# Differential attention: the step's probabilities are turned before the value products and the turned output

## The chip, the cores and the metric

The kernel runs on one core of one Trainium2 chip, as one launch. The metric is the device time of that launch in microseconds. Five engines run their own instruction streams in order and meet through semaphores: PE (TensorE, matrix products; PEld is its weight load), ACT (ScalarE), DVE (VectorE), POOL (GpSimd) and SP (SyncE, which issues the transfers of weights).

## What is computed

The reference is a stack of four blocks on 512 positions with 256 context positions, width 1024. The change lies in the mixer of the second one, differential attention with 8 heads. Each head has two query and key halves m = 0, 1 of 64 columns and one value of 128 columns, and the output uses the difference of the two softmaxes:

```python
def _diff_core(q, k, v, lam, sub_g, lam_init):
    b, nq, h, _, d = q.shape
    s = jnp.einsum('bqhmd,bkhmd->bhmqk', q, k).astype(jnp.float32) * d ** -0.5
    p = jax.nn.softmax(s, axis=-1)
    a = (p[:, :, 0] - lam * p[:, :, 1]).astype(v.dtype)
    o = jnp.einsum('bhqk,bkhe->bqhe', a, v)
    o = _rms_norm(o, sub_g) * (1.0 - lam_init)
    return o.reshape(b, nq, h * v.shape[-1])
```

The keys are the 512 positions and the 256 context positions, 768 in all; the queries are the 512 positions. The output product with `w_out`, the residual and the MLP follow.

## The kernel before

The program is one list of phases (norms, linear layers, attention, scans, fast products), and each engine has a function of its own that walks through it. Weights come through a ring of chunks that SP fills. At the end of the attention phase all engines meet (`end_phase`: each drains and waits for the others), and only then does the next phase, the output product at L1247, begin.

The differential attention is cut into 32 **steps**: a step is one head and one block of 128 queries, with both halves m. For a step j the work is this, and each function below belongs to one engine:

- PE `scores(j)` (L1015): the scores of both halves, 128 x 768 each, into one of three slots of two PSUM banks (banks 0 to 5). With three slots for two halves a step, it waits until `probs(2j-2)` has been read out: `probs_ready` at 2j-1.
- DVE `maxima` (L2034): two reductions to the negated row maximum, one a half, straight from PSUM.
- ACT `probs` (L1474): exponential of a half with its row sum. There are four buffers of probabilities, so `probs(2j)` also waits for `pt_ready`, that is until `turn(j-2)` has read the buffer.
- DVE `inverse` and `mix` (L2043 to L2059): inverses of the sums, and the difference of the two halves (L2054, 128 x 768).
- PE `turn(j)` (L1028): six 128 x 128 transposes of the difference, four into bank 6 and two into the first half of bank 7.
- DVE and ACT `copy_pt(j)`: DVE copies bank 6 out (L2066), ACT the two tiles of bank 7 (L1482).
- PE `values(j)` (L1043): six products with the values, summed in the third quarter of bank 7 (`DIFF_O`).
- ACT `copy_o(j)` (L1494) copies that sum out, and `square_o(j)` (L1503) sums its squares; POOL (L2569, L2571, L2759) takes the inverse root of them and scales the output.
- PE `turn_y(j)` (L1053) transposes the scaled output into the last quarter of bank 7 (`DIFF_Y`); ACT `take_y(j)` (L1512) copies it to its place.

The steps are overlapped by hand. In round j of its loop each engine does the pieces of several steps. ACT's round is `probs(2j)`, `copy_pt(j-2)`, `copy_o(j-3)`, `take_y(j-5)`, `probs(2j+1)`, `square_o(j-3)`. DVE's round is `maxima(2j)`, `maxima(2j+1)`, `copy_pt(j-2)`, `inverse(2j-2)`, `inverse(2j-1)`, `mix(j-1)`. PE's round is the loop that the diff changes. Three of the products' targets share bank 7 and the waits keep PE from writing it while ACT reads it.

Of the kernel before, what the change touches and what calls it, by code (L numbers as in the profile page):

```python
# [236 lines left out]
def build(nc, a, out):  # L237
    PHASES, CHUNKS = plan()
    with ExitStack() as ctx:
# [3 lines left out]
        def sem(name):  # L243
            return ctx.enter_context(nc.semaphore(name))
# [235 lines left out]
        o_ready = sem("o_ready")  # L480
        y_ready = sem("y_ready")
        yt_ready = sem("yt_ready")
        yt_taken = sem("yt_taken")
# [54 lines left out]
        o_copied = sem("o_copied")  # L538
# [308 lines left out]
        def diff_scores(item):  # L847

            h, n, m = item
            rows = slice(64 * m, 64 * m + 64)  # L850
            k, q = KTT[rows, h], QT[rows, h, n * P:(n + 1) * P]
            return q, [(k[:, 0:512], 0), (k[:, 512:T], 512)]

        def diff_values(item):
            return [V1[:, t, item[0] * P:(item[0] + 1) * P] for t in range(6)]
# [7 lines left out]
        def s_slot(i):  # L863
            return psf[:, (i % 3) * 1024:(i % 3) * 1024 + 1024]
# [58 lines left out]
        def _(pe):  # L923
# [79 lines left out]
            def differential():  # L1003
                nv = len(DIFF) // 2

                def scores(j):

                    if j:

                        pe.wait_ge(probs_ready, 2 * j - 1)  # L1010
                    for part in range(2):
                        for i in (2 * j, 2 * j + 1):
                            q, ks = diff_scores(DIFF[i])
                            k, at = ks[part]
                            mm = nc.tensor.matmul(s_slot(i)[:, at:at + k.shape[1]], q, k, start=True, stop=True)  # L1015
                            if part:
                                mm.then_inc(scores_ready, 1)

                def turn(j):

                    pe.wait_ge(probs_mixed, j + 1)
                    if j >= 1:

                        pe.wait_ge(pt_copied_act, j)
                        pe.wait_ge(pt_copied_dve, j)
                    for t in range(6):
                        src = PB[:, 2 * (j % 2), t * P:(t + 1) * P]
                        mm = nc.tensor.transpose(ps[:, PT_BANK[t // 4], (t % 4) * P:(t % 4 + 1) * P], src, ident[:, :])  # L1028
                    mm.then_inc(pt_ready, 1)

                def values(j):
                    vt = diff_values(DIFF[2 * j])

                    pe.wait_ge(pt_copied_act, j + 1)
                    pe.wait_ge(pt_copied_dve, j + 1)
                    if j >= 1:

                        pe.wait_ge(o_copied, j)
                    if j >= 3:

                        pe.wait_ge(yt_taken, j - 2)
                    for t in range(6):
                        mm = nc.tensor.matmul(DIFF_O, PT[:, j % 2, t * P:(t + 1) * P], vt[t], start=t == 0, stop=t == 5)  # L1043
                    mm.then_inc(o_ready, 1)

                def turn_y(y):

                    pe.wait_ge(y_ready, y + 1)
                    if y >= 1:

                        pe.wait_ge(yt_taken, y)
                    pe.wait_ge(o_copied, min(y + 2, nv))
                    nc.tensor.transpose(DIFF_Y, YT[:, y % 2, :], ident[:, :]).then_inc(yt_ready, 1)  # L1053

                for j in range(nv + 5):
                    if j < nv:
                        scores(j)
                    if 3 <= j <= nv + 2:
                        values(j - 3)
                    if 5 <= j:  # L1060
                        turn_y(j - 5)
                    if 2 <= j <= nv + 1:
                        turn(j - 2)

            def norm(i, g, cols):
                n = norm_phases.index(i)
# [279 lines left out]
            for i, ph in enumerate(PHASES):  # L1346
                kind, layer = ph["kind"], ph["layer"]
                if kind in ("norm", "final"):
                    norm(i, ph["groups"][0], ph["cols"])
                elif kind == "linear":  # L1350
                    first = ph["groups"][:NSLOT - 1] if i == first0 + 1 else []
                    if first:
                        together(first)
                    for g in ph["groups"][len(first):]:
                        product(pe, g)
                elif kind == "quick":
                    quick(i, ph)
                elif kind == "attention" and layer == 1:
                    differential()
                elif kind == "attention":  # L1360
                    paired(layer)
                elif kind == "scan":
                    scan(i)
                if kind == "attention" and layer >= 2:
                    pe.drain().then_inc(phase_done, 1)

                    pe.wait_ge(pair_out, pair_base[layer] + 12)
                    early_part(i + 1, 0, range(4, 5), False, False)
                    early_part(i + 1, 1, range(2, 5), True, False)
                    pe.wait_ge(phase_done, 4 * met[i])  # L1370
                else:
                    end_phase(pe, i)
# [4 lines left out]
        def _(act):  # L1377
# [87 lines left out]
            def differential():  # L1465
                nv = len(DIFF) // 2

                def probs(i):

                    act.wait_ge(max_ready, i + 1)  # L1470
                    if i >= 4:

                        act.wait_ge(pt_ready, i // 2 - 1)
                    nc.scalar.activation(PB[:, i % 4, 0:T], s_slot(i)[:, 0:T], ACT.Exp, bias=small[:, i % 4:i % 4 + 1],  # L1474
                                         accum_out=small[:, 4 + i % 4:5 + i % 4]).then_inc(probs_ready, 1)

                def copy_pt(j):
                    act.wait_ge(pt_ready, j + 1)
                    if j >= 2:

                        act.wait_ge(o_ready, j - 1)
                    nc.scalar.activation(PT[:, j % 2, 512:T], ps[:, PT_BANK[1], 0:2 * P], ACT.Copy).then_inc(pt_copied_act, 1)  # L1482

                def copy_o(j):

                    act.wait_ge(o_ready, j + 1)
                    act.wait_ge(pt_ready, min(j + 2, nv))
                    if j >= 2:

                        act.wait_ge(yt_ready, j - 1)  # L1490
                    if j >= 2:

                        act.wait_ge(y_ready, j - 1)
                    nc.scalar.activation(OC[:, j % 2, :], DIFF_O, ACT.Copy).then_inc(o_copied, 1)  # L1494

                def square_o(j):

                    act.wait_ge(o_copied, j + 1)
                    act.wait_ge(root_scale, j + 1)
                    if j >= 2:  # L1500

                        act.wait_ge(o_inv, j - 1)
                    nc.scalar.activation(SUBT, OC[:, j % 2, :], ACT.Square, scale=small[:, 48 + j % 8:49 + j % 8],  # L1503
                                         accum_out=small[:, 20 + j % 2:21 + j % 2]).then_inc(o_squares, 1)

                def take_y(y):

                    act.wait_ge(yt_ready, y + 1)
                    act.wait_ge(pt_ready, min(y + 4, nv))
                    act.wait_ge(o_ready, min(y + 3, nv))  # L1510
                    h, n, _ = DIFF[2 * y]
                    nc.scalar.activation(H[:, h, n * P:(n + 1) * P], DIFF_Y, ACT.Copy, scale=SUBG).then_inc(yt_taken, 1)  # L1512

                for j in range(nv + 5):
                    if j < nv:
                        probs(2 * j)
                    if 2 <= j <= nv + 1:
                        copy_pt(j - 2)
                    if 3 <= j <= nv + 2:
                        copy_o(j - 3)  # L1520
                    if j >= 5:
                        take_y(j - 5)
                    if j < nv:
                        probs(2 * j + 1)
                    if 3 <= j <= nv + 2:
                        square_o(j - 3)
# [1387 lines left out]
```

## Time and profile before

| what | value |
|---|---|
| time, median of 3 runs | 3598.48 us (3594.2 to 3599.9) |
| time of the profiled execution | 3597.63 us |
| its span | 3595.8 us |
| PE, DVE, POOL, ACT busy | 93%, 59%, 43%, 27% of the span |
| the attention phase of the change | about 1248 to 1416 us from the span's start |
| start of the last `scores`, step 31 | 1398.88 us |

The span is the stretch from the first to the last instruction; 1.8 us of the profiled execution lie outside it. PE is busy in most of the program, but the busy share is a mean over phases with different limits, so the attention phase has to be read by itself. All times in the trace are counted from the span's start. An entry of the timeline that gathers several instructions of one kind gives the start of the first and the time from there to the end of the last.

### The profile page before, as it was taken

Reading aid. Unit: us, or ns where it says so; the run is one execution under the profiler, and the core shown is the slowest. Engines: PE = TensorE matmul, PEld = TensorE weight load, DVE = VectorE, ACT = ScalarE, POOL = GpSimd, SP = SyncE. Lnnn points to the kernel's source line nnn. Section 1 sums busy time; section 2 is a strip of 40 time slices with the busy share of each in tenths; the row PEclk is TensorE's granted clock in tenths of the full one; section 3 lists DMA queues with packets and bytes.
Section 4 is the critical chain, followed back from the end, with each engine's and each line's share of the span. In section 5 each row is a group of like instructions: output and inputs, shape, how many; then the busy total and the mean of one; then the engine's idle time right before and its main releaser. Section 6 shows DMA issues by size and latency. Waiting matters only on the chain. (4 is left out here: it accounts for less than half of the span.)

```text
span 3595.8 us, 45001 instructions
## 1 busy us (share of the span) xinstructions
PE 3360.5 (93%) x16256; PEld 2576.4 (72%) x16256; DVE 2119.4 (59%) x3508; ACT 977.1 (27%) x2309; POOL 1529.4 (43%) x1503
## 2 busy tenths in 40 slices
PE   8979999999999977999999978899999988899998
PEld 5665555555546856888888746588888866668887
DVE  7577646544532176455556667478864777645654
ACT  2166210001120054211122264322212345432211
POOL 1044322222221023444454468465645547645654
PEclk9999999999999999999999988999999998999999
DMA  7300223333311100344432200134443200022222
GB/s 248 129 1 7 94 100 117 117 111 117 117 66 53 48 1 13 101 166 161 158 110 82 68 12 9 67 135 155 156 152 98 85 31 16 10 78 90 83 89 82
DMA packets 91099, 317.70 MB, mean 88 GB/s; under 512 B 10816, under 2 KB 13152, under 8 KB 90880
## 3 DMA queue, kind: packets, MB, share of 16 engines
q1 hardware_dynamic: 64224, 218.34, 18.7%
q10 hardware_dynamic: 24768, 90.19, 6.8%
q0 software_dynamic: 1888, 6.29, 0.6%
q8 instruction: 133, 2.18, 0.2%
q14 instruction: 86, 0.70, 0.1%
HBM read 312.68 MB, written 2.10 MB: 88 GB/s over the span
## 5 line engine op out<-in xcount | busy, mean ns | idle before, releaser
L1247 PE MATMUL ps<-arena 128*128 128x256 f32 (+1 forms) x3744 | 951.4, 408 | 2.7 <-DVE arena L2195 2.7
L1247 PEld LDWEIGHTS ps<-arena 128*128 128x128 f32 x3744 | 710.8, 190 | 207.6 <-issue 4.3
L2619 POOL TENSOR_TENSOR arena<-ring,arena 128x512 f32<-128x512 f32 (+1 forms) x140 | 182.5, 1304 | 843.9 <-PE ps L1247 843.9
L1247 PE MATMUL ps<-arena,ring 128*128 128x256 f32 (+1 forms) x1968 | 506.4, 409 | 3.1 <-ACT arena L1582 3.1
L1247 PEld LDWEIGHTS ps<-arena,ring 128*128 128x128 f32 x1968 | 373.3, 190 | 114.6 <-ACT arena L1582 5.9
L1247 PE MATMUL ps<-hbuf,ring 128*128 128x256 f32 (+1 forms) x1696 | 436.6, 412 | 12.2 <-ACT hbuf L1689 10.9
L1247 PEld LDWEIGHTS ps<-hbuf,ring 128*128 128x128 f32 x1696 | 333.3, 197 | 98.0 <-issue 15.3
L2215 DVE TENSOR_TENSOR arena<-ps,arena 128x256 f32<-128x256 f32 (+1 forms) x180 | 80.1, 445 | 340.8 <-PE ps L1247 235.1
L613 PE MATMUL ps<-hbuf,ring 128*128 128x512 f32 x736 | 267.3, 526 | 4.3 <-ACT hbuf L1689 2.5
L2103 DVE CUSTOM_DVE_ANT_0 aring<-aring,csil,adab 128x1024 f32<-128x1024 f32 x176 | 262.3, 1511 | 1.7
L2220 DVE SCALAR_TENSOR_TENSOR resid<-ps,mod,resid 128x256 f32<-128x256 f32 (+2 forms) x296 | 137.4, 482 | 188.6 <-PE ps L1247 184.0
L2602 POOL TENSOR_TENSOR arena<-ring 128x512 f32<-128x512 f32 (+1 forms) x140 | 180.0, 1286 | 156.2 <-PE ps L1247 150.3
L613 PEld LDWEIGHTS ps<-hbuf,ring 128*128 128x128 f32 x736 | 141.3, 193 | 128.6 <-issue 118.8
L2220 DVE SCALAR_TENSOR_TENSOR resid<-arena,mod,resid 128x256 f32<-128x256 f32 (+1 forms) x168 | 109.7, 672 | 206.6 <-ACT arena L1582 203.3
L2613 POOL TENSOR_TENSOR arena<-ring 128x512 f32<-128x512 f32 (+1 forms) x140 | 220.4, 1574 | 0.0
L1582 ACT ACTIVATE arena<-ps 128x256 f32<-128x256 f32 (+1 forms) x140 | 57.6, 411 | 534.3 <-PE ps L1247 534.3
L2683 POOL TENSOR_SCALAR arena<-arena,small 128x512 f32<-128x512 f32 (+2 forms) x144 | 98.8, 698 | 238.7 <-DVE small L1984 238.7
L2608 POOL TENSOR_TENSOR arena<-arena,ring 128x512 f32<-128x512 f32 (+1 forms) x140 | 190.3, 1359 | 18.9 <-issue 0.4
L1575 ACT ACTIVATE arena<-ps 128x256 f32<-128x256 f32 (+1 forms) x168 | 68.2, 406 | 470.2 <-PE ps L1247 460.0
L1247 PE MATMUL ps<-hbuf,arena 128*128 128x256 f32 (+1 forms) x672 | 175.8, 404 | 0.0
L1247 PEld LDWEIGHTS ps<-hbuf,arena 128*128 128x128 f32 x672 | 127.7, 190 | 34.4
L2282 DVE SCALAR_TENSOR_TENSOR arena<-arena 128x512 f32<-128x512 f32 x88 | 141.8, 1611 | 3.1
(300 smaller groups left out, 5164.9 us busy)
## 6 DMA issues: line engine op xcount, KB each, us to landing
aring<-in_ada ACTq DMA_DIRECT2D x172, 512.0 KB, 4.8
ring<-in_mlp SPq DMA_DIRECT2D x128, 512.0 KB, 3.7
ring<-in_up SPq DMA_DIRECT2D x88, 512.0 KB, 3.3
ring<-in_in SPq DMA_DIRECT2D x56, 512.0 KB, 3.2
ring<-in_down SPq DMA_DIRECT2D x32, 512.0 KB, 3.6
ring<-in_odd_in SPq DMA_DIRECT2D x24, 512.0 KB, 3.2
arena<-in_ada SPq DMA_DIRECT2D x16, 512.0 KB, 13.7
ring<-in_out SPq DMA_DIRECT2D x16, 512.0 KB, 3.2
```

The costliest lines, as they stand in the source:

```text
L613: mm = nc.tensor.matmul(slot[:, lo:hi], ring[:, c % RING, k, :], src[:, kt, lo:hi], start=kt == k0, stop=kt == k0 + nkt - 1)
L1247: return nc.tensor.matmul(ps[:, bank, 0:p.tw], w, x, start=start, stop=stop, skip_group_check=True)
L1575: nc.scalar.activation(second_sum(i, n)[:, 0:tw], ps[:, XB[n % 2], 0:tw], ACT.Copy).then_inc(quick_act, 1)
L2103: nc.vector.tensor_tensor_reduce(wt, wt, csil[:, 0, :], 1.0, adab[:, layer, nb:nb + 1], ALU.mult, ALU.add, mod[:, layer, nb, 0:1]).then_in ...
L2215: return nc.vector.tensor_tensor(home(p, half, lo, lo + tw), turned_view(p, product), turned_view(p, kept), ALU.add)
L2220: x = nc.vector.scalar_tensor_tensor(out=X[:, blk, a_:b_], in0=src[:, a_ - lo:b_ - lo], scalar=mod[:, layer, p.gate + blk, s_:s_ + 1], in1 ...
L2282: nc.vector.scalar_tensor_tensor(out=v, in0=u[:, 2:S + 2], scalar=CFW[:, blk, 2:3], in1=v, op0=ALU.mult, op1=ALU.add).then_inc(conv_out, 1)
L2602: nc.gpsimd.tensor_tensor(s[0], f1[:, 0:h], f1[:, h:2 * h], ALU.add).then_inc(wsum_ready, 1)
L2608: nc.gpsimd.tensor_tensor(s[1], s[0], f0[:, 0:h], ALU.subtract).then_inc(wsum_ready, 1)
L2613: nc.gpsimd.tensor_tensor(s[2], f0[:, 0:h], f1[:, 0:h], ALU.subtract).then_inc(wsum_ready, 1)
L2619: nc.gpsimd.tensor_tensor(s[3], f0[:, h:2 * h], s[1], ALU.subtract).then_inc(wsum_ready, 1)
L2683: nc.gpsimd.tensor_scalar(v, v, small[:, 12 + i % 4:13 + i % 4], 1.0, ALU.mult, ALU.mult).then_inc(pair_scaled, 1)
```

## The change

In PE's loop `turn(j - 2)` moves from the end of a round to the place right behind `scores(j)`, ahead of `values(j - 3)` and `turn_y(j - 5)`. No instruction is added or taken away but waits. Since the turned tiles in bank 7 are now written while other parts of the bank may still be unread, `turn(j)` waits as well for `copy_o(j-2)` and `take_y(j-4)` of ACT. And since the value products and the turned output of a round now come behind `turn`, ACT's `copy_pt(j)` waits for `values(j-1)` and `turn_y(j-3)` to be finished before it reads bank 7.

```diff
@@ PE, turn(j)
                         pe.wait_ge(pt_copied_act, j)
                         pe.wait_ge(pt_copied_dve, j)
+                    if j >= 2:
+                        pe.wait_ge(o_copied, j - 1)
+                    if j >= 4:
+                        pe.wait_ge(yt_taken, j - 3)
                     for t in range(6):
@@ PE, the loop
                 for j in range(nv + 5):
                     if j < nv:
                         scores(j)
+                    if 2 <= j <= nv + 1:
+                        turn(j - 2)
                     if 3 <= j <= nv + 2:
                         values(j - 3)
                     if 5 <= j:
                         turn_y(j - 5)
-                    if 2 <= j <= nv + 1:
-                        turn(j - 2)
@@ ACT, copy_pt(j)
                     act.wait_ge(pt_ready, j + 1)
+                    if j >= 1:
+                        act.wait_ge(o_ready, j)
+                    if j >= 3:
+                        act.wait_ge(yt_ready, j - 2)
                     if j >= 2:
                         act.wait_ge(o_ready, j - 1)
```

How one round stands on PE before, in the steady part of the phase (L1015 `scores`, L1043 `values`, L1053 `turn_y`, L1028 `turn`; in brackets what the instruction waits for):

```order
L1015 MATMUL ps<-arena 128x512 [waits probs_ready]
L1015 MATMUL ps<-arena 128x512
L1015 MATMUL ps<-arena 128x256 x2
L1043 MATMUL ps<-arena 128x128 [waits o_copied,yt_taken,pt_copied_dve,pt_copied_act]
L1043 MATMUL ps<-arena 128x128 x5
L1053 MATMUL ps<-ident,arena 128x128 [waits o_copied,yt_taken,y_ready]
L1028 MATMUL ps<-ident,arena 128x128 [waits pt_copied_dve,pt_copied_act,probs_mixed]
L1028 MATMUL ps<-ident,arena 128x128 x5
```

And the same round on PE now (L1034 is `turn`, L1049 `values`, L1059 `turn_y`):

```order
L1015 MATMUL ps<-arena 128x512 [waits probs_ready]
L1015 MATMUL ps<-arena 128x512
L1015 MATMUL ps<-arena 128x256 x2
L1034 MATMUL ps<-ident,arena 128x128 [waits o_copied,pt_copied_dve,yt_taken,pt_copied_act,probs_mixed]
L1034 MATMUL ps<-ident,arena 128x128 x5
L1049 MATMUL ps<-arena 128x128 [waits o_copied,yt_taken,pt_copied_dve,pt_copied_act]
L1049 MATMUL ps<-arena 128x128 x5
L1059 MATMUL ps<-ident,arena 128x128 [waits o_copied,yt_taken,y_ready]
```

The six transposes have gone from the round's end to the place behind the scores, with two more waits; the six value products and the turned output stand behind them. On ACT the order is unchanged. A round there now (L1480 `probs`, L1494 `copy_pt`, L1506 `copy_o`, L1524 `take_y`, L1515 `square_o`):

```order
L1480 ACTIVATE arena,small<-ps,small 128x768 [waits pt_ready,max_ready]
L1494 ACTIVATE arena<-ps 128x256 [waits yt_ready,o_ready,pt_ready]
L1506 ACTIVATE arena<-ps 128x128 [waits yt_ready,y_ready,pt_ready,o_ready]
L1524 ACTIVATE hbuf<-ps,arena 128x128 [waits o_ready,pt_ready,yt_ready]
L1480 ACTIVATE arena,small<-ps,small 128x768 [waits pt_ready,max_ready]
L1515 ACTIVATE arena,small<-arena,small 128x128 [waits o_inv,root_scale,o_copied]
```

Only the second of them has changed: `copy_pt` has `yt_ready` among its waits, and waits for a later count of `o_ready`.

## Rows read from the trace of the kernel before

**Rows 1.** The page: the span, and what the transfers moved in its 40 slices.
```profile
span 3595.8 us, 45001 instructions
GB/s 248 129 1 7 94 100 117 117 111 117 117 66 53 48 1 13 101 166 161 158 110 82 68 12 9 67 135 155 156 152 98 85 31 16 10 78 90 83 89 82
```

**Rows 2.** Stretches: length, busy of PE, PEld, DVE, ACT, POOL, PE clock, transfers.
```profile
1200.00:1250.00 50.00, 48.49 (x429) 47.43 (x427) 5.09 (x6) 0.00 (x0) 0.00 (x0) 1.00 0.15 53
1262.00:1400.00 138.00, 106.03 (x742) 77.29 (x742) 109.33 (x223) 81.41 (x247) 33.42 (x81) 1.00 0.00 1
1418.00:1419.00 1.00, 1.00 (x3) 0.77 (x3) 1.00 (x1) 0.00 (x0) 0.86 (x2) 0.50 0.00 0
```

**Rows 3.** Waits from 1260 to 1410 us: total, times, longest.
```profile
ACT arena L1474 <- PE ps L1028: 60.5, 29, 2.7
PE ps L1015 <- ACT arena L1474: 32.0, 28, 1.1
```

**Rows 4.** Timeline of one round: start us, us, engine, line, operation [idle before].
```profile
1322.81 0.90 ACT L1474 ACTIVATE arena<-ps,small 128x768 f32<-128x768 f32 x1 [2.05 <-PE ps L1028]
1323.70 0.37 ACT L1482 ACTIVATE arena<-ps 128x256 f32<-128x256 f32 x1
1323.86 1.56 PE L1015 MATMUL ps<-arena 64*128 64x512 f32 x8 [1.14 <-ACT arena L1474]
...
1324.12 0.38 ACT L1512 ACTIVATE hbuf<-ps,arena 128x128 f32<-128x128 f32 x1
1324.37 0.92 ACT L1474 ACTIVATE arena<-ps,small 128x768 f32<-128x768 f32 x1
...
1325.35 1.60 PE L1043 MATMUL ps<-arena 128*128 128x128 f32 x12
1325.45 1.82 DVE L2034 TENSOR_REDUCE small<-ps 128x1 f32<-128x768 f32 x2 [0.50 <-PE ps L1015]
...
1325.85 0.23 POOL L2569 TENSOR_SCALAR small<-small 128x1 f32<-128x1 f32 x1 [3.59 <-ACT arena L1503]
...
1326.79 0.27 PE L1053 MATMUL ps<-ident,arena 128*128 128x128 f32 x1
...
1326.83 0.45 POOL L2759 TENSOR_SCALAR arena<-arena,small 128x128 f32<-128x128 f32 x1
1326.90 0.82 PE L1028 MATMUL ps<-ident,arena 128*128 128x128 f32 x6
1327.75 0.69 DVE L2066 COPY arena<-ps 128x512 f32<-128x512 f32 x1 [0.48 <-PE ps L1028]
1327.81 0.90 ACT L1474 ACTIVATE arena<-ps,small 128x768 f32<-128x768 f32 x1 [2.05 <-PE ps L1028]
```

**Rows 5.** Timeline of rounds 2 and 3, before the steady part.
```profile
1257.01 1.82 DVE L2034 TENSOR_REDUCE small<-ps 128x1 f32<-128x768 f32 x2 [0.30 <-PE ps L1015]
1258.01 0.90 ACT L1474 ACTIVATE arena<-ps,small 128x768 f32<-128x768 f32 x1 [1.76 <-DVE small L2034]
1258.75 0.68 DVE L2066 COPY arena<-ps 128x512 f32<-128x512 f32 x1
...
1259.05 1.56 PE L1015 MATMUL ps<-arena 64*128 64x512 f32 x8 [1.26 <-ACT arena L1474]
...
1259.85 1.02 DVE L2054 SCALAR_TENSOR_TENSOR arena<-arena,small 128x768 f32<-128x768 f32 x1
...
1260.85 1.81 DVE L2034 TENSOR_REDUCE small<-ps 128x1 f32<-128x768 f32 x2
```

**Rows 6.** Timeline of the phase's end, from the last scores on.
```profile
1398.88 1.56 PE L1015 MATMUL ps<-arena 64*128 64x512 f32 x8 [1.14 <-ACT arena L1474]
...
1408.16 1.02 DVE L2054 SCALAR_TENSOR_TENSOR arena<-arena,small 128x768 f32<-128x768 f32 x1
1408.33 0.93 POOL L2569 TENSOR_SCALAR small<-small 128x1 f32<-128x1 f32 x1 [1.01 <-ACT arena L1503]
...
1411.33 1.58 PE L1043 MATMUL ps<-arena 128*128 128x128 f32 x12 [0.99 <-ACT hbuf L1512]
```

## The prediction
> **What bounds the kernel now.** I read the slices of the page first: between about 1250 and 1417 us the transfers move 1 GB/s [rows 1, 2], so nothing is fetched that a shorter phase could run into, and no weight stream goes on behind it. Next the stretches: from 1262 to 1400 us PE is busy 106.0 of 138 us, DVE 109.3, ACT 81.4, at a full PE clock [rows 2]. Nobody is full, so a loop through several engines sets the pace. The list of waits names it: ACT's exponential waits 60.5 us in 29 times for the transposes, and PE's scores wait 32.0 us in 28 times for the exponential [rows 3]. These two wait for each other.
>
> The timeline of one round shows the loop [rows 4]. The exponential `probs(2j-2)` starts at 1322.81. The scores follow at 1323.86, 1.05 later; `values` at 1325.35, 1.49 later; `turn_y` at 1326.79, 1.44 later; `turn` at 1326.90, 0.11 later; and the next exponential at 1327.81, 0.91 later (0.82 of transposes and 0.09 to pass the news). Sum 5.00 us, with no slack in it. From the scores of round 3 at 1259.05 [rows 5] to those of round 31 at 1398.88 [rows 6] 28 rounds take 139.83 us, 4.99 each, so the loop holds throughout. The value products and the turned output lie in it though the exponential needs neither.
>
> **What the change does to the loop.** With `turn` right behind the scores the old loop is 1.05 + 1.49 + 0.91 = 3.45 us. What is late next has to be found among these, all from the same rows:
>
> - PE's own work. Every piece remains: 1.49 scores, 0.82 turn, 1.44 values, 0.11 turn_y = **3.86 us** a round.
> - DVE's own work. In round 2 DVE never waits between its first reduction at 1257.01 and the next round's at 1260.85 [rows 5]: **3.84 us**.
> - Scores, maximum, exponential. Scores to reduction 1.59 [rows 4], reduction to exponential 1.00 (1257.01 to 1258.01), exponential to scores 1.05 [rows 4, 5]: 3.64 us.
> - ACT, with its new wait. `copy_pt` can start only behind `turn_y` of the same round: turn start + 0.82 + 1.44 + 0.27 + 0.09 = +2.62. From there `take_y` ends at +0.80 (1323.70 to 1324.12 + 0.38), POOL hears of `square_o` at +2.15 (1323.70 to 1325.85) [rows 4]. The next `turn` waits for `take_y`: 2.62 + 0.80 + some 0.15 = 3.57 us after this one, under the 3.86 of PE. Taken over two rounds, `copy_pt`, the rest of ACT's round (2.15 at most), exponential to scores 1.05, scores 1.49, and 2.62 back to `copy_pt` make 7.31, 3.66 a round. The wait therefore costs nothing as long as rounds take over 3.66; the cover is PE's own next scores. What is queued behind it on ACT is `probs(2j+1)`, which now starts at turn + 3.29 instead of + 2.47; DVE wants its sum 2.4 us into its next round, about two us later.
> - The new waits of `turn`, for `copy_o` and `take_y` of ACT's previous round, are the 3.57 above.
> - The chain through DVE and back. This is the slowest. `mix(j-1)` ends 3.86 behind the first reduction of its round (2.84 + 1.02) [rows 5]; the news takes about 0.09; then `turn` 0.82, `values` 1.44, `turn_y` 0.11, the scores two rounds on, and 1.59 to their reduction: 3.86 + 0.09 + 2.37 + 1.59 = 7.91 for two rounds, **3.955 us** each.
>
> The trace doesn't show how long DVE's word takes to a PE that waits for it here. From PE to ACT it is 0.09, from ACT to PE 1323.86 - 1323.71 = 0.15 [rows 4]. I take 0.09; at zero the chain gives 3.91, at 0.15 3.985. `turn` has more semaphores to wait for; a tenth of a us for that in each `turn` would make it about 4.03.
>
> **The sum.** Up to the scores of round 3 nothing changes: no value product stands ahead of the first `turn`. Round 3: `turn(1)` waits for the mix, which ends at 1259.85 + 1.02 = 1260.87, and starts at 1260.96. It has no turned output yet, so `values` starts at 1261.78 and the scores of round 4 at 1263.22. Carried on by the same offsets, the scores of round 5 stand at 1267.06, of 6 at 1271.13 (now with `turn_y`; `turn(3)` waits for the mix), of 8 at 1279.04, 7.91 later. From 8 on two rounds take 7.91: 11 pairs bring round 30 to 1366.05, and PE's 3.86 bring round 31 to 1369.91. Before it was 1398.88: **28.97 us** gained.
>
> The end of the phase gives a little back. From the last scores to `values(31)` it was 1411.33 - 1398.88 = 12.45 [rows 6]. Now: the reduction at +1.59, `mix(30)` at +5.45, `turn(30)` at 5.54 and its copy on DVE at 6.45; from that copy to the end of the mix 2.12 (1258.75 to 1260.87) [rows 5], 8.57. Meanwhile `values(29)` and `turn_y(27)` end at 8.07, ACT copies from 8.16, `take_y(27)` ends at 8.96, so `turn(31)` starts at about 9.1, `values(30)` at 9.9, `turn_y(28)` at 11.4, ACT's copies at 11.7 to 12.5, `values(31)` at 12.6: **0.2 us** longer. What follows it, the last outputs through POOL, is as before.
>
> Behind the phase stands a meeting of all engines, so the rest of the program moves forward as a block; with the transfers at rest since 1250 us none is late by it. Saved: 28.97 - 0.2 = 28.8 us. The profiled execution took 3597.63, which gives 3568.8; the median of the runs is 0.85 above it, so the forecast is **3569.7 us**, 0.8% faster.
>
> The likeliest case's own range: with PE's 3.86 a round from round 6, its scores at 1271.13 + 25 x 3.86 = 1367.6 and 31.0 us saved, 3567.5; with 4.1 a round, 25 x 0.145 = 3.6 less, 3573.3. With one us for the spread of the runs 3566.5 to 3574.
>
> **The rivals.** A change within 0.2%, 7.2 us, can't be told from none here.
>
> *A part of it lost on DVE.* DVE now has 0.1 us to spare a round instead of some 1.1, so anything that stretches one of its instructions shows. The row that bears on it is POOL's scaling of 1408.33, which took 0.93 instead of 0.23 and ended at 1409.26, just behind DVE's mix of 1408.16 to 1409.18 [rows 4, 6]: the two block each other when they meet. Were POOL first, its last operation of 0.45 [rows 4] could hold DVE's mix or the small product before it. In the steady part POOL starts at turn + 2.62 + 2.15 = 4.77, that is 0.8 into the next round, and ends 1.43 later (1325.85 to 1327.28) at 2.25; the reductions begin within 0.1 of `turn`, and the mix 2.84 behind them. So they miss each other by about 0.6. If they met every round DVE would need 3.84 + 0.45 = 4.29: 25 x 0.335 = 8.4 us lost, 3578. The Trainium skill has this as a rule (SBUF — State Buffer, Who interferes with whom): a VectorE instruction with two SBUF inputs and a GpSimd one that reads SBUF exclude each other for the whole instruction, and the one that issues first wins. By that rule, with every round meeting, it is the 3578 just worked out; the trace agrees on the mix holding POOL and has no case here of POOL holding the mix. Chance 0.10.
>
> *No gain.* Some chain that I didn't see is 5.0 long too, or a cheap wait isn't cheap: it would take 1.3 us more in ACT's group of copies (3.66 to 5.0). Then the time stays at 3597 to 3599. For it: ACT's new wait is a real lengthening of its path. Against it: each engine's busy time a round is under 3.9 and all releases are seen at about 0.1. Chance 0.05.
>
> *Slower.* PE's clock. At half the full clock, which the trace has at 1418 us behind the idle end of this phase [rows 2], PE's 3.86 would be 7.72 and 28 rounds would cost 28 x 2.72 = 76 us more than now: 3675. It decides from a mean granted clock of about 0.77, where 3.86 becomes 5.0. Against it: PE gets busier (77% to some 97%), and from 1200 to 1250 us it was 97% busy at 1.00 [rows 2]. Chance 0.04.
>
> **How the numbers follow.** The likeliest case has 0.81. With the loss on DVE, faster by over 0.2% has 0.91, within it 0.05, slower 0.04. The range of 8 in 10 goes a little below the likeliest case's, for a clock that happens to fall less at the phase's end (up to 2 us), and up to the loss on DVE: 3565 to 3579.
>
> **What would show it.** In the profile after: scores every 3.95 us, with pairs of rounds of 7.9; no wait of the exponential for `turn`, but for the reduction; PE waiting 0.1 to 0.2 us before `turn` for the mix in every second round; ACT's `copy_pt` waiting for `turn_y`; DVE without a pause above 0.1; the meeting at 1387.7. It is wrong if the mix or the reductions grow longer (1.02, and 1.82 for two), if `turn` waits for `take_y`, or if the phase after begins 29 us earlier and the span doesn't shrink by that.

## The result and the profile after

The changed kernel takes 3568.2 us (median of 4 runs, 3563.2 to 3568.7), the kernel before 3596.3 us (4 runs, 3591.0 to 3599.9): a ratio of 0.9921, 95% interval 0.9909 to 0.9933, that is 0.8% faster. The forecast was 3569.7 us, with a range from 3565 to 3579.

The profiled execution took 3568.44 us with a span of 3566.6, against 3597.63 and 3595.8 [rows 1]. The page: its head, the row of the engines' busy times and the row of the transfers.

```profile
span 3566.6 us, 45061 instructions
PE 3367.4 (94%) x16256; PEld 2581.0 (72%) x16256; DVE 2122.7 (60%) x3508; ACT 980.7 (27%) x2309; POOL 1527.4 (43%) x1503
GB/s 250 130 1 2 100 95 118 110 120 114 116 73 53 48 7 31 123 155 166 159 93 84 56 12 11 71 148 148 165 140 101 89 22 18 8 81 89 87 86 82
```

The work is the same, the span is shorter, and the pause of the transfers (slices 14 and 15 of the last row, 7 and 31 against 1 and 13) has become shorter with the phase. The steady stretch of the attention phase in the view by stretches, with the columns of [rows 2]:

```profile
1262.00:1370.00 108.00, 106.17 (x752) 77.57 (x754) 105.95 (x223) 84.26 (x247) 33.55 (x81) 1.00 0.01 1
```

PE is now busy 106.2 of 108 us and DVE 106.0, where it was 106.0 and 109.3 of 138: two engines are full at once. The list of waits in that stretch answers to [rows 3], which is over 150 us where this one is over 108:

```profile
ACT arena L1494 <- PE ps L1059: 13.4, 26, 0.5
PEld ps L1034 <- DVE arena L2066: 13.4, 28, 0.7
ACT arena L1480 <- PE ps L1034: 6.2, 13, 1.7
ACT arena L1480 <- DVE small L2046: 4.1, 15, 0.3
```

The wait of the exponential (now L1480) for `turn` (L1034) has fallen from 60.5 to 6.2 us, and the wait of the scores for the exponential, 32.0 us before, is gone from the list. New are ACT's `copy_pt` (L1494) waiting for `turn_y` (L1059), and `turn`'s weight load waiting for DVE's mix (L2066), 28 times in 28 rounds. Two rounds of the timeline answer to [rows 4]:

```profile
1300.61 1.81 DVE L2046 TENSOR_REDUCE small<-ps 128x1 f32<-128x768 f32 x2
1300.69 0.64 PEld L1034 LDWEIGHTS ps<-ident,arena 128*128 128x128 f32 x6 [0.52 <-DVE arena L2066]
1300.69 0.87 PE L1034 MATMUL ps<-ident,arena 128*128 128x128 f32 x6
...
1301.40 1.50 PE L1049 MATMUL ps<-arena 128*128 128x128 f32 x12
...
1302.74 0.27 PE L1059 MATMUL ps<-ident,arena 128*128 128x128 f32 x1
...
1302.94 1.56 PE L1015 MATMUL ps<-arena 64*128 64x512 f32 x8
...
1303.19 0.38 ACT L1494 ACTIVATE arena<-ps 128x256 f32<-128x256 f32 x1 [0.53 <-PE ps L1059]
...
1303.44 1.02 DVE L2066 SCALAR_TENSOR_TENSOR arena<-arena,small 128x768 f32<-128x768 f32 x1
...
1303.62 0.37 ACT L1524 ACTIVATE hbuf<-ps,arena 128x128 f32<-128x128 f32 x1
...
1304.52 0.88 PE L1034 MATMUL ps<-ident,arena 128*128 128x128 f32 x6
1304.53 1.82 DVE L2046 TENSOR_REDUCE small<-ps 128x1 f32<-128x768 f32 x2
...
1306.77 1.56 PE L1015 MATMUL ps<-arena 64*128 64x512 f32 x8
...
1308.37 1.81 DVE L2046 TENSOR_REDUCE small<-ps 128x1 f32<-128x768 f32 x2
1308.44 0.64 PEld L1034 LDWEIGHTS ps<-ident,arena 128*128 128x128 f32 x6 [0.51 <-DVE arena L2066]
...
1310.70 1.56 PE L1015 MATMUL ps<-arena 64*128 64x512 f32 x8
```

Read it along the two-round chain that the prediction named. The reduction at 1300.61 begins DVE's round. Its mix ends at 1303.44 + 1.02 = 1304.46, `turn` starts 0.06 later, at 1304.52; scores two pieces on at 1306.77, 2.25 later; and the reduction after them begins at 1308.37, 1.60 later: 3.85 + 0.06 + 2.25 + 1.60 = 7.76. The scores stand at 1302.94, 1306.77, 1310.70: rounds of 3.83 and 3.93 in turn, 7.76 the pair. `turn` starts 0.06 behind the end of a mix in the rounds beside this one too (1300.69 and 1308.45): two such chains, one round apart, run side by side. All 28 rounds, from the scores of round 3 at 1260.12 to those of round 31 at 1368.84, take 108.72 us, 3.88 each, against 139.83.

### The profile page after: what moved, and what is told of

It is laid out like the page before. It is cut to its first block and busy times, and to the rows that moved or that the text cites. A ratio compares the mean times of both kernels' runs of the same rounds, so it can differ in the third digit from the quotient of the medians.

```text
span 3566.6 us, 45061 instructions
## 1 busy us (share of the span) xinstructions
PE 3367.4 (94%) x16256; PEld 2581.0 (72%) x16256; DVE 2122.7 (60%) x3508; ACT 980.7 (27%) x2309; POOL 1527.4 (43%) x1503
```

## The experiments

Since the kernel's own time scatters by 5 to 12 us from run to run, which is more than many of the effects, each experiment is read first from the **28 rounds** of its profiled execution (start of the scores of round 3 to those of round 31). This length came out the same to 0.01 us in two executions of the changed kernel, 108.72. The times follow in the table at the end of this section.

**Half of the move.** `turn` ahead of the turned output, but still behind the value products, against the changed kernel:

```diff
-                    if 2 <= j <= nv + 1:
-                        turn(j - 2)
                     if 3 <= j <= nv + 2:
                         values(j - 3)
+                    if 2 <= j <= nv + 1:
+                        turn(j - 2)
                     if 5 <= j:
                         turn_y(j - 5)
```

> Half of the move: turn stands behind the value products and ahead of the turned output only (scores, values, turn, turned output). Loop theory: what counts is how much work stands between an exponential and the turn that frees the next one; here only the turned output's 0.11 us leaves the loop, so a round goes from 5.00 to 4.89, 28 rounds save about 3 us against the kernel before (a ratio of 0.999). Rival, that the new waits or the new order as such bring the gain: some 28 us. Rival, that ACT's new wait costs by itself: no gain, or slower.

The 28 rounds took 137.02 us, 4.89 each, 2.8 less than before. The ratio is 0.9991 (0.9981 to 1.0). One of the waits of the timeline in it:

```profile
1320.59 0.90 ACT L1480 ACTIVATE arena<-ps,small 128x768 f32<-128x768 f32 x1 [1.94 <-PE ps L1034]
```

The exponential still waits 1.94 us for `turn` (2.05 before, [rows 4]). The 0.10 a round is what the turned output's 0.11 us ahead of `turn` is worth; it leaves nothing for the new waits or the new order as such. In the whole time so small a gain is hardly shown: the ratio's interval ends at 1.0.

**Work that nobody needs, on DVE.** The same edit in both kernels:

```diff
+                    nc.vector.tensor_copy(JUNK[:, (j % 2) * 512:(j % 2) * 512 + 512], ps[:, PT_BANK[0], 0:512])
                     nc.vector.tensor_copy(PT[:, j % 2, 0:512], ps[:, PT_BANK[0], 0:512]).then_inc(pt_copied_dve, 1)
```

> The kernel before, and DVE copies bank 6 once more in each step (into scratch), 0.60 us of work a round that nobody needs. Loop theory: DVE has 1.16 us to spare in the round of 5.00, so the time stays within 1 us of before. Rival, that DVE's work always counts: 28 x 0.6 = 17 us slower.

> The changed kernel with the same additional copy on DVE. Loop theory: DVE's own round of 3.84 becomes 4.44 and sets the pace, against 3.88 now: 28 x 0.56 = 16 us slower than the changed kernel, that is 12 to 13 us faster than before. Rival, that some chain without DVE sets the pace with slack on DVE: clearly less than 16 us.

In the kernel before the 28 rounds stayed at 139.83 us. In the changed one they took 124.21, 4.44 each (4.425 once settled), 15.5 more than 108.72. Here `turn` keeps PE waiting for the mix:

```profile
1324.07 0.87 PE L1034 MATMUL ps<-ident,arena 128*128 128x128 f32 x6 [0.61 <-DVE arena L2066]
```

The same 0.60 us is free in one kernel and costs 0.55 a round in the other. The missing 0.05 is what the chain lay above DVE's own round: 3.88 against 3.83.

**Half of the value products** left out, again in both:

```diff
-                    for t in range(6):
-                        mm = nc.tensor.matmul(DIFF_O, ..., start=t == 0, stop=t == 5)
+                    for t in range(0, 6, 2):
+                        mm = nc.tensor.matmul(DIFF_O, ..., start=t == 0, stop=t == 4)
```

> The kernel before with three of the six value products of a step left out (the output leaves out half of the keys). Loop theory: they stand in the loop, 0.66 to 0.72 us less a round, 28 rounds: 18 to 20 us faster than before. Rival, that the waits for exponentials come from elsewhere: no change.

> The changed kernel with three of the six value products of a step left out (the output leaves out half of the keys). DVE's own round of 3.84 stays, so by the chain theory a round goes from 3.88 to 3.84 and only 1 us is saved, against some 17 in the kernel before. Rival, that PE's own work sets the pace of the changed kernel: 28 x 0.67 = 19 us faster than it.

Before: 121.08 us for the 28 rounds, 18.8 less than 139.83, 0.67 a round. After: 107.28, 1.4 less than 108.72, rounds of 3.83. PE's stream is then 0.67 us a round shorter, and only 0.05 a round comes of it, so PE's own stream isn't the bound in the changed kernel. What is left, 3.83, is DVE's own round. Now PE waits twice in each round, for the exponential ahead of the scores and for the mix ahead of `turn`:

```profile
1319.85 1.56 PE L1015 MATMUL ps<-arena 64*128 64x512 f32 x8 [0.36 <-ACT arena L1480]
1321.66 0.88 PE L1034 MATMUL ps<-ident,arena 128*128 128x128 f32 x6 [0.25 <-DVE arena L2066]
```

**ACT's new wait.** One and two more copies on ACT, behind the wait that the change adds:

```diff
+                    nc.scalar.activation(JUNK[:, (j % 2) * 256:(j % 2) * 256 + 256], ps[:, PT_BANK[1], 0:2 * P], ACT.Copy)
                     nc.scalar.activation(PT[:, j % 2, 512:T], ps[:, PT_BANK[1], 0:2 * P], ACT.Copy).then_inc(pt_copied_act, 1)
```

> The changed kernel, and ACT copies its two tiles of bank 7 once more in each step (into scratch), 0.28 us behind ACT's new wait. By the profile of the changed kernel copy_pt starts 2.50 us behind turn and take_y frees the next turn at 3.44, while a round takes 3.88. Chain theory (mix to turn through DVE sets the pace): 3.44 + 0.28 = 3.72 is still under 3.88, no change, 0 to 1 us. Rival, that ACT's new wait sets the pace: 28 x 0.28 = 8 us slower than the changed kernel.

> The same with two additional copies on ACT, 0.55 us. Chain theory: 3.44 + 0.55 = 3.99 is now over 3.88 and ACT sets the pace by 0.11, some 3 us slower than the changed kernel. Rival, that ACT's wait sets the pace already: 15 us slower. Rival, that ACT has over half a us to spare: no change.

With one more the 28 rounds took 108.73 us, with two more 111.12, rounds of 3.97 once settled. With two `turn` waits for `take_y`, as worked out:

```profile
1323.71 0.84 PE L1034 MATMUL ps<-ident,arena 128*128 128x128 f32 x6 [0.19 <-ACT hbuf L1526]
```

So ACT's new wait costs nothing in the changed kernel, and its margin lies between 0.28 and 0.55 us; 3.97 says some 0.45.

**Less work on DVE.** It copies two of its four tiles:

```diff
-                    nc.vector.tensor_copy(PT[:, j % 2, 0:512], ps[:, PT_BANK[0], 0:512])
+                    nc.vector.tensor_copy(PT[:, j % 2, 0:256], ps[:, PT_BANK[0], 0:256])
```

> The changed kernel, DVE copies two of the four tiles of bank 6 (the output leaves out the other two's right values). 0.27 us less on DVE in a round: DVE 3.57, the chain mix to turn (7.76 - 0.27) / 2 = 3.75, PE 1.49 + 0.71 + 1.34 + 0.20 = 3.74. Chain theory: rounds of 3.75, 28 x 0.13 = 4 us faster than the changed kernel. Rival, that PE's work is 3.86 as predicted and sets the pace: within 1 us. Rival, that DVE's work alone sets it: 28 x 0.27 = 8 us faster.

104.90 us, 3.746 a round: as expected, 3.8 less than the changed kernel. That is 0.13 a round for the 0.27 taken away. It rules out both rivals of the expectation: PE's work isn't 3.86, and DVE's own round (now 3.57) doesn't set the pace alone. It can't tell the chain (3.745) from PE's own stream (3.74), though, since the two tie here:

```profile
1314.12 1.56 PE L1015 MATMUL ps<-arena 64*128 64x512 f32 x8
1314.54 1.02 DVE L2066 SCALAR_TENSOR_TENSOR arena<-arena,small 128x768 f32<-128x768 f32 x1
1315.61 0.88 PE L1034 MATMUL ps<-ident,arena 128*128 128x128 f32 x6
```

`turn` starts 1.49 behind the scores, which is the scores' own length on PE, and at the same time 0.05 behind the end of the mix at 1315.56. A further cut on DVE alone should therefore bring nothing more; no run tried it.

**The mix ahead of the copy** in DVE's round:

```diff
-                    if 2 <= j <= nv + 1:
-                        copy_pt(j - 2)
                     if 1 <= j <= nv:
                         inverse(2 * j - 2)
                         inverse(2 * j - 1)
                         mix(j - 1)
+                    if 2 <= j <= nv + 1:
+                        copy_pt(j - 2)
```

> The changed kernel, and in DVE's round inverse and mix come ahead of the copy of the turned tiles. The mix ends 0.6 us earlier, so the chain mix to turn falls to about 3.58, but DVE's own round of 3.84 stays. Chain theory: rounds of 3.84 instead of 3.88, 1 us faster than the changed kernel, if the later copy still comes ahead of the value products (by 0 to 0.1 us, so a few hundredths may be lost again). Rival, that the changed kernel's pace is PE's own work: exactly as the changed kernel, 3.88.

This expectation failed: 111.96 us, 4.00 a round, 3.2 more than the changed kernel. Once settled the rounds alternate between 3.83 and 4.16. The rows:

```profile
1318.49 0.68 DVE L2078 COPY arena<-ps 128x512 f32<-128x512 f32 x1
...
1319.36 0.64 PEld L1034 LDWEIGHTS ps<-ident,arena 128*128 128x128 f32 x6 [0.41 <-issue]
1319.38 1.82 DVE L2046 TENSOR_REDUCE small<-ps 128x1 f32<-128x768 f32 x2 [0.20 <-PE ps L1015]
...
1321.66 1.02 DVE L2066 SCALAR_TENSOR_TENSOR arena<-arena,small 128x768 f32<-128x768 f32 x1
...
1322.66 0.68 DVE L2078 COPY arena<-ps 128x512 f32<-128x512 f32 x1
1323.26 1.81 DVE L2046 TENSOR_REDUCE small<-ps 128x1 f32<-128x768 f32 x2
...
1323.55 0.85 PE L1034 MATMUL ps<-ident,arena 128*128 128x128 f32 x6 [0.38 <-issue]
```

The mix ends at 1322.68, but `turn` starts only at 1323.55, 0.21 behind the end of the copy at 1323.34. I had left out that `turn` also waits for `pt_copied_dve` of the step ahead, because it writes the bank that the copy reads. The rows name no engine for this wait (`issue`). That it is the copy's word is read from the code and from the time, which is nearly the same one round earlier (0.19, from 1318.49 + 0.68 to 1319.36). With that in place of the mix the chain, added up from this run's own rows, is 3.96 + 0.21 + 2.25 + 1.59 = 8.01 for two rounds, and 8.00 was measured: it closes without slack. It stands as one more sign that DVE's word to `turn` sets the pace, whichever instruction gives it. Why the word takes 0.21 here and 0.06 behind the mix is open.

**A better share of the copies.** DVE takes two tiles, ACT the other four in one instruction across both banks, behind DVE's:

```diff
 ACT, copy_pt(j)
                     act.wait_ge(pt_ready, j + 1)
+                    act.wait_ge(pt_copied_dve, j + 1)
-                    nc.scalar.activation(PT[:, j % 2, 512:T], ps[:, PT_BANK[1], 0:2 * P], ACT.Copy)
+                    nc.scalar.activation(PT[:, j % 2, 256:T], psf[:, PT_BANK[0] * 512 + 256:PT_BANK[0] * 512 + 768], ACT.Copy)
 DVE, copy_pt(j)
-                    nc.vector.tensor_copy(PT[:, j % 2, 0:512], ps[:, PT_BANK[0], 0:512])
+                    nc.vector.tensor_copy(PT[:, j % 2, 0:256], ps[:, PT_BANK[0], 0:256])
```

> The changed kernel, and the copy of the turned tiles is shared out anew: DVE takes two of the six tiles, ACT four in one instruction across banks 6 and 7, behind DVE's. The same reference output is computed. DVE 3.57 a round, the chain (7.76 - 0.27) / 2 = 3.75, PE 3.74, ACT's way back to turn 3.44 + 0.27 = 3.71. Chain theory: rounds of 3.75, 4 us faster than the changed kernel, 0.9% faster than before. Rival, that ACT has no room for 0.27 us more: rounds of 3.9 to 4.0, slower than the changed kernel.

> The changed kernel once more, as the control on the same chip for the two others: 0.992 of before, rounds of 3.88.

The 28 rounds took 105.09 us, 3.753 each, 3.6 less than the control's 108.72 (the changed kernel once more). As with the smaller copy, the chain and PE's own stream tie at this length: in a settled round the scores start at 1322.18, `turn` at 1323.67, 1.49 later, and the mix ends at 1323.61. The two pieces of the copy in a row:

```profile
1321.76 0.41 DVE L2079 COPY arena<-ps 128x256 f32<-128x256 f32 x1
...
1322.44 0.60 ACT L1495 ACTIVATE arena<-ps 128x512 f32<-128x512 f32 x1 [0.44 <-PE ps L1059]
```

In the whole time it doesn't show: 3566.4 us (3565.4 to 3566.8) against the control's 3568.2 (3560.8 to 3571.9), and the same ratio to before, 0.9917. The phase is shorter as expected; that the kernel is faster isn't shown by these runs.

Each ratio of the table is to runs of the kernel before that were taken beside it (their medians lie between 3594.3 and 3598.5), so the medians of two rows don't compare to better than some 4 us.

| kernel | 28 rounds, us | a round | median, us | ratio to before (95%) |
|---|---|---|---|---|
| before | 139.83 | 4.99 | 3596.3 | |
| changed | 108.72 | 3.88 | 3568.2 | 0.9921 (0.9909 to 0.9933) |
| turn between values and turned output | 137.02 | 4.89 | 3592.0 | 0.9991 (0.9981 to 1.0) |
| before, DVE copy twice | 139.83 | 4.99 | 3596.7 | 1.0009 (0.9999 to 1.0019) |
| changed, DVE copy twice | 124.21 | 4.44 | 3583.8 | 0.9966 (0.9954 to 0.9979) |
| before, half of the values | 121.08 | 4.32 | 3577.6 | 0.9946 (0.9931 to 0.9961) |
| changed, half of the values | 107.28 | 3.83 | 3559.8 | 0.9911 (0.9881 to 0.9941) |
| changed, ACT copy twice | 108.73 | 3.88 | 3563.7 | 0.9913 (0.9884 to 0.9942) |
| changed, ACT copy thrice | 111.12 | 3.97 | 3567.2 | 0.9923 (0.9894 to 0.9952) |
| changed, DVE copies half | 104.90 | 3.75 | 3557.7 | 0.9896 (0.9868 to 0.9925) |
| changed, mix ahead of the copy | 111.96 | 4.00 | 3569.5 | 0.9926 (0.9913 to 0.9939) |
| changed, ACT takes two tiles more | 105.09 | 3.75 | 3566.4 | 0.9917 (0.9903 to 0.9930) |
| changed, once more | 108.72 | 3.88 | 3568.2 | 0.9917 (0.9903 to 0.9931) |

## Why the prediction was right

The time came out 1.5 us from the forecast. The mechanism is the one that was predicted, but that the number is so close is in part luck: the phase became 2.4 us shorter than predicted, and 2.0 us of what it gained didn't reach the span.

- **The loop of before.** Right. Taking 0.11 us of the turned output out of it gave 0.10 a round, taking half of the value products out gave 0.67, and work on DVE beside it cost nothing.
- **What is late next: the chain through DVE and back, two rounds long.** Right in kind, a little long in size: I had 7.91 us for two rounds and it is 7.76. The term "`turn` 0.82, `values` 1.44, `turn_y` 0.11" came out as 0.71, 1.34 and 0.20, 2.25 together where I had 2.37. The 0.82 of [rows 4] was a time to the end of the last transpose, but the next piece doesn't wait for that end: in the profile after the six transposes last to 1300.69 + 0.87 = 1301.56 and `values` starts at 1301.40. The other two were taken from start to start, but from pieces with other neighbours. Before, the value products stood behind the scores, and their first product is recorded together with its weight load (PEld at 1325.34, PE at 1325.35); now they stand behind `turn`, and it is recorded 0.11 behind the load:

```profile
1301.29 1.42 PEld L1049 LDWEIGHTS ps<-arena 128*128 128x128 f32 x12
1301.40 1.50 PE L1049 MATMUL ps<-arena 128*128 128x128 f32 x12
```

`turn_y` has the scores behind it instead of `turn`, 0.20 in place of 0.11. DVE's word to PE takes 0.06, where I took 0.09. Together 0.15 in two rounds.
- **PE's own 3.86.** Too long by the same terms: 1.49 + 0.71 + 1.34 + 0.20 = 3.74. It didn't matter, since the chain lies above it; the experiment with half of the value products rules out PE as the bound of the changed kernel. With less work on DVE it would be the next one.
- **DVE's own 3.84.** Right: 4.425 with 0.60 added is 3.83, and 3.83 was left when PE had half its products to do.
- **ACT's new wait, at nothing.** Right: one more copy behind it is free, two are not. I had `take_y` free the next `turn` at 3.57, and it is 1303.19 - 1300.69 + 0.80 + 0.14 = 3.44.
- **The sum.** Predicted 110.86 us for the 28 rounds, measured 108.72. The end of the phase: predicted 12.6 us from the last scores to the last value products, measured 1381.22 - 1368.84 = 12.38, before 12.45, so it gave nothing back. From the first scores to the first product of the next phase it was 1416.48 - 1248.03 = 168.45 us and is 1386.38 - 1249.10 = 137.28, **31.2 us** less, where I had 28.8.
- **"The rest of the program moves forward as a block".** True in kind only to 2 us: of the 31.2 the profiled spans keep 29.2. The attention phase itself began 1.07 us later, though nothing ahead of it was changed, and the rest was lost behind it. The phase behind began 1416.48 - 1386.38 = 30.1 us earlier and the span shrank by 29.2, so 0.9 us of the last sign of being wrong did come. What takes these 2 us is open. The granted clock stood at 0.93 from 200 to 250 us in that execution and at 0.98 in the one of before, and the control (0.93, its phase begins at 1249.25) fits that. But the run with half of the values begins its phase at 1249.96 with 0.98 there, and the one with ACT's copy thrice at 1250.13 with 0.97, so that row doesn't explain it alone.
- **The rivals.** POOL and DVE blocking each other didn't happen in the steady part: POOL ends its round at 1302.84 and DVE's small product starts at 1303.19, 0.35 later, the mix 0.60. Where POOL and the mix do meet, at the end of the phase, the mix isn't longer for it, so no run shows the 0.45 us a round that I put on this rival; the last section has the rows. No piece of a round turned out to be 5.0 long, and the granted clock of the phase stayed at 1.00 with PE at 98%.
- **Signs that I named.** The exponential was to wait no more for `turn`: it does in every second round, for 0.33 us. It costs little, since the reduction would have let it go only 0.05 earlier (1300.61 + 1.00 = 1301.61, and it starts at 1301.66). PE was to wait for the mix in every second round: by PE's own gaps it does (0.12 ahead of 1308.45), but `turn` follows the mix by 0.06 in both. The meeting came at 1386.4, not 1387.7, in a phase that began 1.07 later.

## What to carry to other kernels

In a pipeline written out by hand, look at what stands between a buffer's reader and the writer that it frees: moving the freeing piece ahead of 1.5 us of work that nobody waits for took 1.1 us from each of 28 rounds here, though no work was saved. Then cost the new round by every engine's own sum and by each chain that crosses engines, those over two rounds too, and take each offset from start to start on one engine, not from start to end of the last instruction, and be ready for a tenth of a us when a piece gets other neighbours. An experiment meant to tell two bounds apart has to be sized so that they don't tie. And before swapping two instructions, write down every semaphore that both raise: a copy that frees a bank may be as urgent as the result one wants earlier.

## What the runs showed of the hardware

**A low clock in some executions.** Up to the scores of round 1 all the kernels do the same work. Yet in the changed kernel with half of the value products the scores of round 1 took 2.93 us in place of 1.56:

```profile
1253.00:1253.50 0.50, 0.00 (x0) 0.00 (x0) 0.45 (x1) 0.50 (x2) 0.00 (x0) 1.00 0.00 0
1254.00:1256.00 2.00, 2.00 (x6) 0.90 (x8) 0.00 (x0) 0.55 (x2) 0.00 (x0) 0.50 0.00 0
1253.72 2.93 PE L1015 MATMUL ps<-arena 64*128 64x512 f32 x8 [2.20 <-ACT arena L1480]
```

From 1254 to 1256 us the granted clock was 0.50, the 1.2 GHz level. It fell after 1253.5, when PE had been without work since 1251.52. In the profile of the changed kernel PE is without work for the same 2.20 us there (1250.66 to 1252.86), and the clock stays at 1.00. The run with ACT's copy thrice has the same late round (5.00 us from the scores of round 1 to those of round 2, 3.63 elsewhere), the other eleven don't. What decides isn't shown. One such place moves all that follows by 1.37 us, which is why the rounds were counted from round 3 on.

**POOL and DVE.** At the end of the phase they do meet, and POOL pays, even when its instruction is recorded as the first by 0.04 us (the control has the same pair at 1376.46 and 1376.51):

```profile
1376.33 1.23 POOL L2771 TENSOR_SCALAR arena<-arena,small 128x128 f32<-128x128 f32 x1
1376.37 1.02 DVE L2066 SCALAR_TENSOR_TENSOR arena<-arena,small 128x768 f32<-128x768 f32 x1
```

POOL's 0.45 became 1.23 and DVE's 1.02 stayed. In no trace here is a mix longer than 1.04 us, not even where POOL is clearly the first: in the run with the mix ahead of the copy POOL's scaling starts 0.33 ahead of a mix, and neither is longer than usual.

```profile
1317.16 0.47 POOL L2771 TENSOR_SCALAR arena<-arena,small 128x128 f32<-128x128 f32 x1
1317.49 1.02 DVE L2066 SCALAR_TENSOR_TENSOR arena<-arena,small 128x768 f32<-128x768 f32 x1
```

So the loss that the prediction priced, POOL holding the mix, was never seen. POOL can hold DVE all the same. The phase behind this one shows it, with longer instructions of POOL (changed kernel):

```profile
1408.34 1.27 POOL L2620 TENSOR_TENSOR arena<-arena,ring 128x512 f32<-128x512 f32 x1
1408.97 0.91 DVE L2232 SCALAR_TENSOR_TENSOR resid<-arena,mod,resid 128x256 f32<-128x256 f32 x1 [3.32 <-ACT arena L1594]
1409.56 1.45 POOL L2591 TENSOR_TENSOR arena<-arena 128x512 f32<-128x512 f32 x1
1409.92 0.48 DVE L2232 SCALAR_TENSOR_TENSOR resid<-ps,mod,resid 128x256 f32<-128x256 f32 x1
```

The first of DVE's two, with both large inputs in SBUF, has a median of 0.48 and took 0.91 while POOL's ran; the second reads one of them from PSUM and stayed at 0.48 beside POOL.
